# The four early adaLN blocks in column groups on TensorE, and the gate rows between the key blocks

## The reference

```python
mod = (silu(c) @ ada_w + ada_b)        # 6 x 1024 values for each of two streams
sh1, sc1, g1, sh2, sc2, g2 = mod
h = rmsnorm(x, norm1_w) * (1.0 + sc1) + sh1
z = h @ w_in + b_in                    # xa, ga | q, k, v, o | i, f (4 + 4 gate columns)
ya = rglru(z xa, z ga)                 # causal conv, gates, linear scan
yb = mlstm(q, k, v, o, i, f)           # f through log_sigmoid, cumulative sums, running maxima
x = x + g1 * (concat(ya, yb) @ w_out)
h2 = rmsnorm(x, norm2_w) * (1.0 + sc2) + sh2
x = x + g2 * peer(h2)                  # for each row and each of 8 heads 16 of 16384 experts
y = rmsnorm(x, final_norm_w)
```

## Time and profile before

| | us |
|---|---|
| median of 3 runs | 3383.03 (3381.96 to 3384.57) |
| the profiled execution | 3386.47 |
| its span in the profile | 3384.7 |
| TensorE busy | 2904.7 (86%) |
| VectorE busy | 2240.8 (66%) |
| ScalarE busy | 2150.0 (64%) |
| GpSimd busy | 1206.0 (36%) |

### The profile page before, as it was taken

One profiled execution on the slowest core, in us unless ns is written; L12 is line 12 of the kernel. 1 busy time (PEld: TensorE's weight loads), 2 busy tenths in 40 slices (PEclk: granted clock), 3 DMA queues, 4 the chain that ended last, 5 costly groups with the idle time before them and its releaser, 6 DMA issues. The chain is left out here.

```text
span 3384.7 us, 42049 instructions
## 1 busy us (share of the span) xinstructions
PE 2904.7 (86%) x9250; PEld 1405.0 (42%) x9250; DVE 2240.8 (66%) x5479; ACT 2150.0 (64%) x7214; POOL 1206.0 (36%) x1134
## 2 busy tenths in 40 slices
PE   7999899788888888888888888887888888888876
PEld 3665455434433444343344434343433344434321
DVE  5675456567676667666666676666666766676665
ACT  2232033377777777777767777776677777777775
POOL 0001010244444444444434443444444344444443
PEclk9999999999999999999999999999999999999999
DMA  6322031699999999999999999999999999999998
GB/s 245 111 95 86 26 109 59 272 419 414 420 417 417 399 419 414 418 399 419 392 418 407 419 415 394 419 416 376 403 419 419 416 396 419 419 406 403 419 419 328
DMA packets 169994, 1191.54 MB, mean 352 GB/s; under 512 B 20026, under 2 KB 21466, under 8 KB 30210
## 3 DMA queue, kind: packets, MB, share of 16 engines
q0 software_dynamic: 155792, 1118.53, 80.5%
q1 hardware_dynamic: 13940, 70.23, 5.5%
HBM read 1179.42 MB, written 9.25 MB: 351 GB/s over the span
## 5 line engine op out<-in xcount | busy, mean ns | idle before, releaser
L912 PE MATMUL ps<-r_w,r_yT 128*128 128x512 f32 (+1 forms) x3168 | 1522.7, 614 | 336.8 <-ACT r_yT L1235 333.6
L1807 DVE SCALAR_TENSOR_TENSOR r_yT<-r_w,r_qk 128x1024 bf16<-128x1024 f32 x792 | 969.0, 1225 | 683.8 <-DMA r_w<-in_peer_uv,gidx 682.2
L587 POOL DMA_INDIRECT r_w<-in_peer_uv,gidx x792 | 872.8, 1102 | 1020.8 <-PE ps L912 879.9
L912 PEld LDWEIGHTS ps<-r_w,r_yT 128*128 128x128 f32 (+1 forms) x3168 | 551.1, 189 | 1224.8 <-issue 1222.8
L912 PE MATMUL ps<-r_yT 128*128 128x512 f32 (+1 forms) x1056 | 527.6, 634 | 85.4 <-ACT r_yT L1235 75.7
L587 POOL DMA_INDIRECT r_yT<-in_peer_uv,gidx x264 | 290.7, 1101 | 559.5 <-PE ps L912 493.2
L1227 ACT ACTIVATE mixc<-mixc 128x1 f32<-128x1 f32 x1056 | 207.2, 196 | 444.0 <-DVE r_yT L1807 440.2
L1235 ACT ACTIVATE r_yT<-ident,mixc 128x128 f32<-128x128 f32 x1024 | 411.2, 402 | 97.7 <-ACT mixc L1231 5.5
L1231 ACT ACTIVATE mixc<-mixc 128x1 f32<-128x1 f32 x1056 | 409.2, 387 | 35.0
L1230 ACT ACTIVATE mixc<-mixc 128x1 f32<-128x1 f32 x1056 | 408.3, 387 | 33.8
L1807 DVE SCALAR_TENSOR_TENSOR r_yT<-r_yT,r_qk 128x1024 bf16<-128x1024 f32 x264 | 323.0, 1225 | 123.0 <-DMA r_yT<-in_peer_uv,gidx 107.4
(11 more groups left out here) (292 smaller groups left out, 2341.1 us busy)
## 6 DMA issues: line engine op xcount, KB each, us to landing
r_w<-in_ada_w SPq DMA_DIRECT2D x18, 1024.0 KB, 5.3
r_w<-in_peer_uv,gidx POOLq DMA_INDIRECT x792, 13.8
r_w<-in_w_lin SPq DMA_DIRECT2D x16, 512.0 KB, 5.0
r_yT<-in_peer_uv,gidx POOLq DMA_INDIRECT x264, 11.8
r_vo<-in_x_prompt SPq DMA_DIRECT2D x8, 512.0 KB, 6.5
r_qk<-in_ada_w SPq DMA_DIRECT2D x2, 2048.0 KB, 18.1
r_w<-in_w_vo SPq DMA_DIRECT2D x2, 2048.0 KB, 7.8
r_w<-in_w_out SPq DMA_DIRECT2D x2, 2048.0 KB, 8.9
```

The source lines that it names most:

```text
L587: pool.indirect_dma_start(ring[place(h, j)], None, table, bass.IndirectOffsetOnAxis(gidx_t[:, h, j:j + 1], 0))\
L912: mm = nc.tensor.matmul(ps[0:r, 2 * p + c, :], diag[:, j % 4, 0:r], row[:, D + c * 512:D + (c + 1) * 512], start=h == 0 and j == 0, stop=h ...
L1807: V.scalar_tensor_tensor(udump[j % 2], ring[i][:, 0:D], 1.0, h2[:, t, :], ALU.mult, ALU.mult, accum_out=dots[:, i:i + 1]).then_inc(dot_don ...
```

## The change

All four early adaLN blocks are made on TensorE, in four column groups: group j holds the same two weight columns and takes 128 of the 512 columns, so that a block is 32 matmuls and its result lies in partitions 32j and 32j+1. Block 3 is read from the two halves in place. Its part on VectorE, the sum and `pick2` are gone; `mod_row` is four additions. SP loads block 3 behind blocks 1 and 2; the halves of block 4 wait for TensorE's fourth block (`ada_mm` 4). The counts of `half_done` are one less.

The gate rows' matmuls stand behind k1, ahead of k2, on TensorE and on ScalarE, and count for three groups (`unit`) there. GpSimd copies the f rows ahead of its waits for the modulation's stores, and VectorE waits for `z_mm` 45.

The order of the units begins (1, 1), (0, 0), (0, 1), (1, 0): the gate unit of the first prompt tile, then the sample's. The first waits only for `wo`. `wv` is loaded at `z_mm` 51, which is now the end of k3.

```diff
-        units = [(i, n) for i in range(NT - 2) for n in range(2)] + [(i, n) for n in range(2) for i in (NT - 2, NT - 1)]
+        VO, ZIF = 51, 45
+        units = [(1, 1), (0, 0), (0, 1), (1, 0)] + [(i, n) for i in range(2, NT - 2) for n in range(2)] + [
+            (i, n) for n in range(2) for i in (NT - 2, NT - 1)]
...
             def load_halves(b):
...
-                    if b >= 4:
-                        sp.wait_ge(half_done[i], b - 3)
+                    if b == 4:
+                        sp.wait_ge(ada_mm, 4)
+                    elif b >= 5:
+                        sp.wait_ge(half_done[i], b - 4)
...
-            load_halves(3)
             load_block(1)
             load_block(2)
+            load_halves(3)
...
-                    sp.wait_ge(z_mm, 48)
+                    sp.wait_ge(z_mm, VO)
...
+            pool.wait_ge(z_ev, ZIF)
+            pool.dma_start(fro, zif[H_B:2 * H_B, :]).then_inc(f_ld, 16)
             for s in range(2):
                 pool.wait_ge(mod_st[s], 128)
...
-            pool.wait_ge(z_ev, 51)
-            pool.dma_start(fro, zif[H_B:2 * H_B, :]).then_inc(f_ld, 16)
...
             def ada_block(b):
-                pe.wait_ge(ada_ld[b], 16)
+                if b < 3:
+                    pe.wait_ge(ada_ld[b], 16)
                 if b >= 2:
                     pe.wait_ge(mod_ev, b - 1)
-                out = ps[0:2, b % 2, :]
                 for k in range(KD):
-                    m = nc.tensor.matmul(out, csil[:, :, k], ada[b][:, k, :], start=k == 0, stop=k == KD - 1)
+                    if b == 3 and k % 4 == 0:
+                        pe.wait_ge(half_ld[k // 4], 16)
+                    w = ada[b][:, k, :] if b < 3 else ada_half[k // 4][:, k % 4, :]
+                    for j in range(4):
+                        m = nc.tensor.matmul(ps[32 * j:32 * j + 2, b % 2, 0:P], csil[:, :, k], w[:, j * P:(j + 1) * P],
+                                             start=k == 0, stop=k == KD - 1)
                 m.then_inc(ada_mm, 1)
...
             ada_block(2)
+            ada_block(3)
             pe.wait_ge(x_evd, NT)
             pe.wait_ge(x_eva, NT)
-            ada_sum(3)
...
+                if b == "k1":
+                    pe.wait_ge(ld_prm, 16)
+                    bank = z_bank()
+                    for k in range(KD):
+                        for j in range(4):
+                            m = nc.tensor.matmul(ps[32 * j:32 * j + 8, bank, 0:QT], wif[:, k, :],
+                                                 hT[:, k, j * QT:(j + 1) * QT], start=k == 0, stop=k == KD - 1)
+                    m.then_inc(z_mm, 3)
+                    unit[0] += 2
...
-                if bank == 6 and j == 5:
-                    pe.wait_ge(lg_ev, 24)
+                if j == 6:
+                    pe.wait_ge(mod_ev, 12)
                 if prior:
-                    pe.wait_ge(z_ev, VO + max(prior[-1] + 1, 2))
+                    pe.wait_ge(z_ev, VO + (3 if prior[-1] == 1 else prior[-1] + 1))
...
+                if j == 0:
+                    pe.wait_ge(vo_ld[1], 16)
                 if i == 0:
                     pe.wait_ge(vo_ld[0], 16)
-                    pe.wait_ge(vo_ld[1], 16)
...
-                if j != 1:
+                if j != 2:
                     value_gate(j)
...
+                if b == "k1":
+                    act.wait_ge(lru_y, 2 * FT)
+                    act.wait_ge(z_mm, unit + 3)
+                    for j in range(4):
+                        m = nc.scalar.activation(zif[:, j * QT:(j + 1) * QT], ps[32 * j:32 * j + 8, unit % 4, 0:QT],
+                                                 ACT.Identity, bias=bif[32 * j:32 * j + 8])
+                    m.then_inc(z_ev, 3)
+                    unit += 3
...
-                row = ps[0:2, 7 if b == 3 else b % 2, :]
-                V.tensor_tensor(modrow[:, b, :], row, abias[:, b, :], ALU.add).then_inc(mod_ev, 1)
+                for j in range(4):
+                    c = slice(j * P, (j + 1) * P)
+                    m = V.tensor_tensor(modrow[:, b, c], ps[32 * j:32 * j + 2, b % 2, 0:P], abias[:, b, c], ALU.add)
+                m.then_inc(mod_ev, 1)
...
-            ada_part(3)
             for b in range(1, 4):
                 mod_row(b)
...
-            dve.wait_ge(z_mm, 48)
+            dve.wait_ge(z_mm, ZIF)
```

More of the change, by code:

```diff
@@ L210, in build @@
         epsc = col(1)
-        pick2 = col(4)
         sel32 = col(DEC)
@@ L336, in project_bank @@
             return 2 + c if i == NT - 1 else 0 if (i, c) == (NT - 2, 1) else 6 + c
-        VO = 51
-        units = [(i, n) for i in range(NT - 2) for n in range(2)] + [(i, n) for n in range(2) for i in (NT - 2, NT - 1)]
+        VO, ZIF = 51, 45
+        units = [(1, 1), (0, 0), (0, 1), (1, 0)] + [(i, n) for i in range(2, NT - 2) for n in range(2)] + [
+            (i, n) for n in range(2) for i in (NT - 2, NT - 1)]
         vo_bank = [(3, 6, 7, 2)[j % 4] for j in range(14)] + [7, 6, 7, 6]
@@ L417, in _ @@
                 if n:
-                    sp.wait_ge(half_done[0], 9)
-                    sp.wait_ge(half_done[1], 9)
+                    sp.wait_ge(half_done[0], 8)
+                    sp.wait_ge(half_done[1], 8)
                 else:
-                    sp.wait_ge(z_mm, 48)
+                    sp.wait_ge(z_mm, VO)
                 sp.dma_start(dst, A["w_vo"][n].rearrange("p (k n) -> p k n", k=KD)).then_inc(vo_ld[n], 16)
@@ L597, in ada_block @@
             def ada_block(b):
-                pe.wait_ge(ada_ld[b], 16)
+                if b < 3:
+                    pe.wait_ge(ada_ld[b], 16)
                 if b >= 2:
                     pe.wait_ge(mod_ev, b - 1)
-                out = ps[0:2, b % 2, :]
                 for k in range(KD):
-                    m = nc.tensor.matmul(out, csil[:, :, k], ada[b][:, k, :], start=k == 0, stop=k == KD - 1)
+                    if b == 3 and k % 4 == 0:
[4 more added lines that the diff above has]
+                                             start=k == 0, stop=k == KD - 1)
                 m.then_inc(ada_mm, 1)
             def ada_sum(b):
[L608 to L617, removed]
+                pe.wait_ge(half_done[1], b - 3)
+                pe.wait_ge(mod_ev, b)
+                for j in range(4):
+                    m = nc.tensor.matmul(ps[32 * j:32 * j + 32, 7, 0:256], ones[:, 0:32],
+                                         acc[j % 2][:, 256 * (j // 2):256 * (j // 2) + 256], start=True, stop=True)
                 m.then_inc(ada_mm, 1)
@@ L728, in value_gate @@
                     pe.wait_ge(z_ev, 48 if bank == 3 else VO)
+                if j == 0:
+                    pe.wait_ge(vo_ld[1], 16)
                 if i == 0:
                     pe.wait_ge(vo_ld[0], 16)
-                    pe.wait_ge(vo_ld[1], 16)
                     for k in range(KD):
-                        for j in range(4):
-                            m = nc.tensor.matmul(ps[32 * j:32 * j + 32, bank, 0:256], hT[:, k, SEQ:T],
-                                                 (wv, wo)[j // 2][:, k, 256 * (j % 2):256 * (j % 2) + 256],
+                        for q in range(4):
+                            m = nc.tensor.matmul(ps[32 * q:32 * q + 32, bank, 0:256], hT[:, k, SEQ:T],
+                                                 (wv, wo)[q // 2][:, k, 256 * (q % 2):256 * (q % 2) + 256],
                                                  start=k == 0, stop=k == KD - 1)
@@ L1288, in _ @@
             V.tensor_tensor(csil, cT, ce, ALU.mult).then_inc(c_silu, 1)
-            link(V.memset(pick2, 0.0))
-            link(V.memset(pick2[:, 0:1], 1.0))
-            link(V.memset(pick2[:, 3:4], 1.0))
             link(V.memset(epsc, EPS))
@@ L1350, in ada_part @@
             def ada_part(b):
-                if b >= 4:
-                    dve.wait_ge(ada_mm, b)
+                dve.wait_ge(ada_mm, b)
                 for k in range(KD):
@@ L1370, in ada_part @@
                         m.then_inc(half_done[i], 1)
-                        dve.wait_ge(half_done[i], b - 2)
+                        dve.wait_ge(half_done[i], b - 3)
                         ch.need()
@@ L1477, in evict_unit @@
                         p = slice(64 * n + 32 * q, 64 * n + 32 * q + 32)
-                        z, b = ps[p, vo_bank[0], 0:256], bvo[p, n, 256 * q:256 * q + 256]
+                        z, b = ps[p, vo_bank[1], 0:256], bvo[p, n, 256 * q:256 * q + 256]
                         if n == 0:
@@ L1513, in _ @@
             dve.wait_ge(ld_wri, 32)
-            dve.wait_ge(z_ev, 51)
+            dve.wait_ge(z_ev, VO)
             evict_vo(0)
```

## The result

The changed kernel took 3362.99 us in the median of 5 runs (3359.38 to 3368.7), the kernel before 3384.57 beside it. The ratio is 0.994 with a 95% interval of 0.9929 to 0.9951: faster by 0.5 to 0.7%. The forecast was 3363.6. The profiled execution took 3363.62, its span is 3361.8, 22.9 less than before.

What follows compares the result with a forecast made beforehand. TensorE bounds the first stage of about 630 us, the DMA engines the 2,750 us gather. Gains of 14.6 and 4.85 sum to 19.4 us, taking the median from 3383.03 to 3363.6; own range 3359 to 3371, 8 in 10 3358 to 3372.

Steps and rivals of the forecast that it cites:

- The early part: Start of the kernel, four adaLN blocks in column groups: first projection matmul at 42.95 instead of 57.54, gain 14.6 us.
- the second part: Behind the key blocks, gate rows earlier and gate unit first: next matmul at 346.95 instead of 351.80, gain 4.85 us.
- the clock: TensorE's idle ahead of the fifth unit 8.7 us, before 8.77, so the lower clock behind it keeps its length.
- The blocks: Early adaLN blocks on TensorE: 0.111 us a step of four groups, 1.78 us per block, 0.2 of drain.
- a sign of being wrong: Early blocks: wrong if TensorE waits for a half of block 3, landing at 34.5 to 36.7, read from 37.5.
- The rival of groups that don't overlap: Early blocks: each weight load waits for the matmul under way, 12.4 us a block; 3406, slower; chance 0.03.
- The gate rows: Behind the second key block: evicted by 295.0, slack 1.2 us, no stall; log-sigmoid starts 3.75 us earlier.
- The step that failed: Ahead of the sample's unit: value weights take 8.0 us, there at 327.8; TensorE idles 1.2 in place of 4.35.
- the second part gives nothing: Rival at the key blocks: a later LRU output stalls ScalarE and TensorE; 14.6 alone, 3368.4; chance 0.08.
- The gather: Expert gather behind the first stage: 2,750 us at the DMA engines' rate, starting some 19 us earlier with the same length.

Runs made afterwards that it cites:

- run 1: The changed kernel measured once more, nothing altered: 3362.75 us, ratio 0.9946 to the kernel before.
- run 7: Changed kernel with ScalarE's Exp of the forget rows behind the third key block's evictions, not the fourth's: 3363.18 us, ratio 0.9939.
- run 2: Kernel before with only the early adaLN blocks in column groups; gate rows, GpSimd's order and units as before: 3367.70 us, ratio 0.9955.
- run 4: Changed kernel with early adaLN blocks in two column groups of 256 columns in place of four of 128: 3366.31 us, ratio 0.9954.
- run 5: Changed kernel with GpSimd's ten stores of the LRU states held until the value weights have landed: 3361.97 us, ratio 0.9933.
- run 6: Kernel before with GpSimd's sample-state loads and ten stores moved ahead of its wait for the gate rows: 3394.81 us, ratio 1.0025.
- run 3: Changed kernel with the early adaLN blocks taken back; only gate rows earlier and gate unit first: 3374.87 us, ratio 0.9977.
- run 9: Changed kernel with adaLN blocks taken back and the ten stores held behind the value weights: 3373.52 us, ratio 0.9973.
- run 8: Changed kernel with Exp behind the third key block and the ten stores behind the value weights: 3351.41 us, ratio 0.9903.

## Why the prediction was right, and where it wasn't

**The early part was right in its mechanism. The total was right in part by luck: the second part gained almost nothing where I had its gain, and a gain of the clock that I hadn't forecast stood in for it.**

*The blocks.* Forecast 1.78 us a block plus drain, measured 1.93 with it; a step of four groups is (1.93 - 0.27)/15 = 0.111 us, the value taken from the gate rows. VectorE's four additions took 1.18 (forecast 1.1) and the wait ahead of the last tile 0.29 (0.2). Block 3 waited 0.3 us for its last half, where I had counted on 0.8 to 3 us of slack and had named such a wait as a sign of being wrong. In the seven profiles with the new order of loads this half landed between 34.8 and 37.6, so the early part has little slack there; the wait cost 0.2 us here (3.85 for blocks 2 and 3, 3.68 in run 1) and 2.0 in run 7. Block 0 took 2.03 and not 3.0: the clock was at 1.00 there in this execution, where the earlier trace rows had 0.51. This 1 us made up for a start 0.8 later. From the first projection to the last sum ahead of the gate rows 1.4 us were lost again to a longer stretch of low clock (0.50 from 42.2 to 49), and at the key blocks the reverse, 1.3: 14.6 forecast, 14.4 measured at their end. The part alone gave 15.5 in the medians (run 2).

*The rival of groups that don't overlap* is dead by the same rows and by run 4. By the rule of the Trainium skill that I weighed ("TensorE: Matmul & The Clock Gate", Part 3), a block would have taken 12 us; it took 1.93. The measurement decides: loads into another column group don't wait for running matmuls.

*The gate rows.* ScalarE evicted them right behind the last LRU output; TensorE idled 0.23 for it (forecast none, slack 1.2: the gate rows were done earlier than I had them, at the higher clock, so that the third key block's second group met its wait sooner). The log-sigmoid began 3.8 us earlier against the key blocks (forecast 3.75).

*The step that failed* is the value weights: "took 8.0 from the end of the last key block to the start of the sample's unit". I carried the duration of a load over to a place where other DMAs were under way. I named the waits that GpSimd's copy is moved past, and didn't ask what stood behind the copy: the ten stores, going out 39 us earlier. Runs 5 and 6 show them to be the cause, from both sides. So the second part gave not 4.85 at the fifth unit but 0.2 in the first profile and 3.1 in the second; where the load doesn't come last it gives 5.2 (runs 3, 5 and 9).

*What made up for it* is the clock, which I had kept as it was. Between the fifth unit and the rows' transposes the same work took 51.2 us before and 48.2 after. Windows of the kernel before show why (columns as in the earlier trace rows):

```profile
352.00:357.60 5.60, 5.60 (x7) 2.32 (x8) 5.20 (x12) 0.41 (x1) 0.00 (x0) 0.50 0.00 0
357.60:402.00 44.40, 44.40 (x105) 19.58 (x104) 19.69 (x63) 5.97 (x8) 1.55 (x3) 1.00 0.00 1
```

5.6 us at the lower level cost half of that, 2.8. In the changed kernel the low stretch lay in the idle and the sample's unit and had ended at 328.9, ahead of the fifth (windows):

```profile
316.00:328.90 12.90, 4.50 (x44) 2.54 (x48) 12.56 (x11) 0.00 (x0) 0.00 (x0) 0.50 0.41 128
328.90:337.10 8.20, 8.20 (x40) 3.69 (x33) 7.73 (x17) 0.00 (x0) 0.00 (x0) 1.00 0.00 0
```

Another such stretch at 405 cost the kernel before 1.7 us and the changed one nothing. A third, of 6.8 us, falls into the sample's output projection in both kernels, but in the changed one it begins earlier against that work and so ends sooner in it; that is 1.3 us. The last 2.3 us of the difference lie in the gather. The 22.9 are thus 14.4 at the key blocks, 0.2 from the unit order, 3.0 + 1.7 + 1.3 from the clock and 2.3 from the gather.

The rival "the second part gives nothing" was right in number at the fifth unit and wrong in mechanism: ScalarE's wait cost 0.2 us. The gather kept its length but for what varies anyhow: 2753.9 us before (630.8 to 3384.7) and 2751.6 after (610.2 to 3361.8), where the eleven profiles have 2750.2 to 2753.9. It begins in the eighth of the page's forty slices, not from the seventh on, as the prediction reads the earlier trace rows.

## What to carry over

When an instruction is moved up in an engine's list, everything queued behind it is released too: list those that follow up to the next wait, and ask which transfers they will meet. A wait that grows can hide behind another: an idle that stays equal in sum, or a fix that gives nothing, calls for taking both away at once, as run 8 did. Here float32 matmuls with two weight columns gained nearly the full factor of four from column groups of 128 columns: 1.93 us a block against 7.03.

## What the runs showed of the hardware

Ten stores with 4-byte elements, 16 KB in all, hold up later transfers long after their own packets are over. In the changed kernel their packets of 96 and 128 bytes lasted 0.1 us on average and 0.2 at most, and the last began at 293.6; yet a load of 2 MB issued 10.6 to 14.5 us after the last store was issued took 13.7 to 20.2 us in six executions, in place of 7.3 to 8.0 in the five in which the stores came behind it, and a copy of 16.5 KB 13.3 in place of 2.1 to 3.4. The slow stretch ends when the last store lands: in the five executions with both times the load lands 5.8 to 6.9 us behind it. The stores need that long by themselves: up to 26.4 us too in the kernel before, with no such load under way. The Trainium skill ("DMA: Bandwidth & Descriptors", Specifications) says that transfers below 512 bytes are done by read-modify-write; whether that is what makes these writes end so late no trace here shows.

Matmuls in four column groups start within 0.03 us of one another with 2 and with 8 weight columns, and a set costs 0.111 us for 128 columns, 0.216 for two groups of 256 ((3.62 - 0.38)/15) and 0.225 for four of 264.

The granted clock of the same instructions differs between executions: the kernel before and run 3 are the same for TensorE up to 285 us, yet block 0 took 8.23 us in one and 7.25 in the other. A forecast from one profile can be off by some microseconds for that alone.
